# Mixed values through four buffers, two in PSUM and two in SBUF, and GpSimd's low parts of the weights in eight pieces

## What is computed

```python
h = rms_norm(x, g)
h_prev = pad(h)[:, :-1];  hh = h_prev - h
xr, xw, xk, xv, xa, xg = (h + hh * mu[i] for i in range(6))
r = xr @ w_r;  k = xk @ w_k;  v = xv @ w_v
w = -softplus(-(w0 + tanh(xw @ w1) @ w2)) - 0.5
a = sigmoid(a0 + (xa @ a1) @ a2)
g = sigmoid(xg @ g1) @ g2
kk = k * k_k, normalised by head;  k = k * (1 + (a - 1) * k_a)
```

## Time and profile before

| | us |
|---|---|
| median of three runs | 2355.26 |
| the runs | 2349.63, 2355.26, 2356.2 |
| profiled execution | 2347.22 |
| its span | 2345.3 |

### The profile page before, as it was taken

The page is one execution under the profiler, slowest core; times in us unless marked ns, Lnnn a source line. Parts: engine busy times, 40 slices in busy tenths (PEclk is TensorE's granted clock), DMA queues, the critical chain, the costliest instruction groups (busy, mean ns, idle before and its releaser), DMA issues.

```text
span 2345.3 us, 36157 instructions
## 1 busy us (share of the span) xinstructions
PE 2057.7 (88%) x15556; PEld 1574.6 (67%) x15556; DVE 848.4 (36%) x1209; ACT 809.4 (35%) x1051; POOL 686.6 (29%) x198
## 2 busy tenths in 40 slices
PE   4687886667999999989998789999998999979997
PEld 2564766663678888866665457888887886747764
DVE  5578443323342221033646724222101234252333
ACT  4566323323243342132124534434212423232232
POOL 1141322201234434423220023343443423203430
PEclk8898899997799999999997879999999998989999
DMA  4111100002123332222110012333323221112110
GB/s 146 36 36 48 41 4 4 4 4 65 46 80 90 94 100 88 98 69 97 54 54 19 1 37 80 98 89 94 99 99 103 79 66 36 54 59 90 54 54 36
DMA packets 190703, 147.06 MB, mean 63 GB/s; under 512 B 6889, under 2 KB 188352, under 8 KB 190577
## 3 DMA queue, kind: packets, MB, share of 16 engines
q1 hardware_dynamic: 190576, 145.18, 20.2%
HBM read 143.06 MB, written 2.10 MB: 62 GB/s over the span
## 4 chain that ended last, share of the span: by engine, by line
PE 76%; DVE 12%; ACT 6%; issue 4%; POOL 1%; DMA 1%; SPq 0%; DVEq 0%; ACTq 0%
PE psum L2296 20%; PE psum L2298 19%; PE psum L2297 19%; PE psum L2459 4%; DVE X_lo L1670 2%; PE psum L2372 1%; ACT w_hi L1149 1%; PE psum L2721 1%; DVE xf L1796 1%; PE psum L2302 1%; PE psum L2684 1%; POOL w_lo L1017 1%; DVE col L2071 1%; PE psum L2878 1%; ACT xf L1181 1%
## 5 line engine op out<-in xcount | busy, mean ns | idle before, releaser
L1017 POOL TENSOR_TENSOR w_lo<-weight_raw,w_hi 128x2048 fp32r<-128x2048 f32 (+2 forms) x134 | 600.7, 4484 | 1384.9 <-ACT w_hi L1149 1384.7
L2296 PE MATMUL psum<-X_hi,w_hi 128*128 128x512 f32 x1528 | 630.7, 413 | 60.4 <-DVE X_lo L1670 42.2
L2298 PE MATMUL psum<-X_hi,w_lo 128*128 128x512 f32 x1528 | 606.0, 397 | 0.0
L2297 PE MATMUL psum<-X_lo,w_hi 128*128 128x512 f32 x1528 | 605.5, 396 | 0.0
L2296 PEld LDWEIGHTS psum<-X_hi,w_hi 128*128 128x128 f32 x1528 | 293.5, 192 | 173.6 <-issue 94.4
L1149 ACT ACTIVATE w_hi<-weight_raw 128x2048 fp32r<-128x2048 f32 (+2 forms) x134 | 249.5, 1863 | 367.0 <-PE psum L2298 356.2
L2297 PEld LDWEIGHTS psum<-X_lo,w_hi 128*128 128x128 f32 x1528 | 293.8, 192 | 64.0 <-issue 6.7
L2298 PEld LDWEIGHTS psum<-X_hi,w_lo 128*128 128x128 f32 x1528 | 293.0, 192 | 64.2
L1719 DVE TENSOR_TENSOR sgate<-rt,psum 128x512 f32<-128x512 f32 x44 | 30.2, 687 | 320.5 <-PE psum L2298 320.5
L2296 PE MATMUL psum<-hb_hi,w_hi 128*128 128x512 f32 x352 | 136.9, 389 | 0.0
L2297 PE MATMUL psum<-hb_lo,w_hi 128*128 128x512 f32 x352 | 136.9, 389 | 0.0
(11 more groups left out here) (439 smaller groups left out, 2702.0 us busy)
## 6 DMA issues: line engine op xcount, KB each, us to landing
weight_raw<-in_ffn_w_gu SPq DMA_DIRECT2D x88, 512.0 KB, 4.9
weight_raw<-in_l_w_in SPq DMA_DIRECT2D x45, 512.0 KB, 4.7
weight_raw<-in_ffn_w_down SPq DMA_DIRECT2D x40, 512.0 KB, 3.6
weight_raw<-in_kv_w SPq DMA_DIRECT2D x16, 512.0 KB, 4.0
weight_raw<-in_l_w_out SPq DMA_DIRECT2D x16, 512.0 KB, 4.0
weight_raw<-in_rw_w_k SPq DMA_DIRECT2D x8, 512.0 KB, 6.7
weight_raw<-in_rw_w_r SPq DMA_DIRECT2D x8, 512.0 KB, 4.1
weight_raw<-in_rw_w_v SPq DMA_DIRECT2D x8, 512.0 KB, 4.5
```

The costliest lines, as they stand in the source:

```text
L1017: ins = pool.tensor_tensor(l, r, h.bitcast(F32), ALU.subtract)
L2296: pe.matmul(ps, wh, xh, start=start, stop=False, skip_group_check=True)
L2297: pe.matmul(ps, wh, xl, start=False, stop=False, skip_group_check=True)
L2298: return pe.matmul(ps, wl, xh, start=False, stop=stop, skip_group_check=True)
```

## The change

Two things change.

1. Mixed values before `y` (the inputs of k, r, g1 and v) and the ring's go through one set of four buffers, `mixed_at(i)`: PSUM bank 6, `xf[:, 0]`, PSUM bank 7, `xf[:, 1]`, by i modulo 4. `ring_f` is gone. The waits are relaxed to match: a buffer of tile i is free with the low part of tile i − 4. ScalarE writes the first halves two tiles ahead, and `ring_first(0)` and `ring_first(1)` stand before `keys_out(0)`. The jobs `second` and `kinv` move from banks 6 and 7 to banks 4 and 5.
2. GpSimd's subtraction for each weight slot is issued as pieces: eight of 256 columns for a full slot (six for one of 1536; eight of 160 or of 128 where the slot has three dimensions). Only the last piece counts the semaphore up, so TensorE waits for all of them. This holds for all slots, the hardware loops included.

```diff
@@ make_jobs
-        j.add(("second", m), 6 + m % 2, "A")
+        j.add(("second", m), 4 + m % 2, "A")
...
-        j.add(("kinv", k), 6 + k % 2, "D")
+        j.add(("kinv", k), 4 + k % 2, "D")
@@ new function
+def pieces(r):
+
+    if len(r.shape) == 3:
+        return [r[:, k:k + 1, :] for k in range(r.shape[1])]
+    return [r[:, c:c + 256] for c in range(0, r.shape[1], 256)]
@@ new function in build
+        def mixed_at(i):
+
+            return (psum[:, 6, :], xf[:, 0, :], psum[:, 7, :], xf[:, 1, :])[i % 4]
@@ low
-                for i, (r, h, l) in enumerate(parts):
-                    ins = pool.tensor_tensor(l, r, h.bitcast(F32), ALU.subtract)
+                for i, part in enumerate(parts):
+                    for r, h, l in zip(*(pieces(q) for q in part)):
+                        ins = pool.tensor_tensor(l, r, h.bitcast(F32), ALU.subtract)
@@ x_high1 and x_low1
+                if src is None:
+                    f = mixed_at(k) if v < XV["y"] else xf[:, k % 2, :]
+                else:
+                    f = src[:, k, :]
@@ mix_first
-                if i >= 2:
-                    act.wait_ge(xlo_ready, i - 1)
-                act.activation(xf[:, i % 2, :], h_sb[:, k, 1:S + 1], ACT.Copy,
+                if v == 1 and k < 4:
+                    act.wait_ge(ring_xl, 2 * KT - 3 + k)
+                elif i >= 4:
+                    act.wait_ge(xlo_ready, i - 3)
+                act.activation(mixed_at(k), h_sb[:, k, 1:S + 1], ACT.Copy,
@@ mix_high
                 mix_first(v, mu, 0)
+                mix_first(v, mu, 1)
                 for k in range(KT):
-                    if k + 1 < KT:
-                        mix_first(v, mu, k + 1)
+                    if k + 2 < KT:
+                        mix_first(v, mu, k + 2)
@@ ring_first
-                if j >= RING:
-                    act.wait_ge(ring_xl, j - RING + 1)
+                if j < 4:
+                    act.wait_ge(xlo_ready, KT - 3 + j)
+                else:
+                    act.wait_ge(ring_xl, j - 3)
-                act.activation(ring_f[j % RING][:, :], h_sb[:, j % KT, 1:S + 1], ACT.Copy,
+                act.activation(mixed_at(j), h_sb[:, j % KT, 1:S + 1], ACT.Copy,
@@ ring_high
-                if j + 1 < 2 * KT:
-                    ring_first(j + 1)
+                if j + 2 < 2 * KT:
+                    ring_first(j + 2)
@@ ScalarE's order
             ring_first(0)
+            ring_first(1)
             keys_out(0)
@@ split
-                    if 8 * v + k >= 2:
-                        dve.wait_ge(xlo_ready, 8 * v + k - 1)
-                    produce(k, xf[:, (8 * v + k) % 2, :]).then_inc(xf_ready, 1)
+                    if 8 * v + k >= 4:
+                        dve.wait_ge(xlo_ready, 8 * v + k - (3 if v < XV["y"] else 1))
+                    produce(k, mixed_at(k) if v < XV["y"] else xf[:, k % 2, :]).then_inc(xf_ready, 1)
```

More of the change, by code:

```diff
@@ L632, in build @@
         first_hi, first_lo = b_("first_hi", [P, KT, P], F32R), b_("first_lo", [P, KT, P], F32R)
-        ring_f = [b_(f"ring_f{i}", [P, S]) for i in range(2)]
         b_ = here(u0_at)
         ring_hi, ring_lo = b_("ring_hi", [P, RING, S], F32R), b_("ring_lo", [P, RING, S], F32R)
-        ring_f += [b_("ring_f2", [P, S])]
         b_ = here(rf_at + size([P, 2, S], F32))
@@ L1166, in x_high1 @@
                     act.wait_ge(kstep, xv_last_k(v - 1, k))
-                act.activation(X_hi[:, k, :], src[:, k, :] if src is not None else xf[:, (8 * v + k) % 2, :],
-                               ACT.Copy).then_inc(xhi_ready, 1)
+                if src is None:
+                    f = mixed_at(k) if v < XV["y"] else xf[:, k % 2, :]
+                else:
+                    f = src[:, k, :]
+                act.activation(X_hi[:, k, :], f, ACT.Copy).then_inc(xhi_ready, 1)
             def x_high(v, src=None):
@@ L1300, in ring_high @@
                     wait_ring_used(act, j - RING)
-                act.activation(ring_hi[:, j % RING, :], ring_f[j % RING][:, :], ACT.Copy).then_inc(ring_xh, 1)
+                act.activation(ring_hi[:, j % RING, :], mixed_at(j), ACT.Copy).then_inc(ring_xh, 1)
             def low_rank(n, func):
@@ L1668, in x_low1 @@
                 dve.wait_ge(xhi_ready, xready(v, k))
-                f = src[:, k, :] if src is not None else xf[:, (8 * v + k) % 2, :]
+                if src is None:
+                    f = mixed_at(k) if v < XV["y"] else xf[:, k % 2, :]
+                else:
+                    f = src[:, k, :]
                 dve.tensor_tensor(X_lo[:, k, :], f, X_hi[:, k, :].bitcast(F32), ALU.subtract).then_inc(xlo_ready, 1)
@@ L1842, in ring_low @@
                 dve.wait_ge(ring_xh, j + 1)
-                dve.tensor_tensor(ring_lo[:, j % RING, :], ring_f[j % RING][:, :], ring_hi[:, j % RING, :].bitcast(F32),
+                dve.tensor_tensor(ring_lo[:, j % RING, :], mixed_at(j), ring_hi[:, j % RING, :].bitcast(F32),
                                   ALU.subtract).then_inc(ring_xl, 1)
@@ L1851, in _ @@
             for j in range(2 * KT):
-                f, mu = ring_f[j % RING], 8 * (MU_W, MU_A)[j // KT] + j % KT
+                f, mu = mixed_at(j), 8 * (MU_W, MU_A)[j // KT] + j % KT
                 dve.wait_ge(ring_half, j + 1)
-                dve.scalar_tensor_tensor(out=f[:, :], in0=h_sb[:, j % KT, 0:S], scalar=pcol("rw_mu", mu), in1=f[:, :],
+                dve.scalar_tensor_tensor(out=f, in0=h_sb[:, j % KT, 0:S], scalar=pcol("rw_mu", mu), in1=f,
                                          op0=ALU.mult, op1=ALU.add).then_inc(ring_mixed, 1)
```

## The result

Five runs of the changed kernel have a median of 2336.82 us (2331.47 to 2339.69); the kernel before, run beside them and counted with the runs shown ahead of the prediction, has 2349.63 (2345.78 to 2356.2). The ratio is 0.9937, 95% interval 0.9913 to 0.996: about 15 us faster (9 to 20 by the interval; the medians are 12.8 us apart). The profiled executions are 2347.22 before and 2339.69 after, 7.5 us apart; the one before is faster than the median of every series of the kernel before, and the one after is the slowest of its five.

The account below looks back on a forecast made before the run. TensorE is busy 88% of 2345.3 us, so only its waits can be won; early −31.8, late −10.4 and piece cost +25.9 sum to −16.3 us: 2331 against the profiled execution, 2339 us on the median, range 2326 to 2361.

Parts of the forecast that it names:

- Start: Before the first product: DVE's three tiny instructions and h_sb tiles get in between pieces, first product at 40.2, −4.4 us.
- First step of k: Product k's first step: two tiles further ahead, mixed tiles come every 1.43 us instead of 2.28, −3.2 us.
- Ring waits: TensorE's three waits for ring_lo, 24.4 us together: −3.8 for the first, −7.5 for the other two, leaving 13.
- Product r: Product r, where DVE and GpSimd are both full: −5.2 us by its end, from mixed tiles made two ahead.
- the rival of the saturated stretch: Early stretch already full, DVE 32.99 of 35 us in r; gains given back, no change, 2356 us; chance 0.15.
- g1 and v: Products g1 and v: shorter tile pitches and, in v, xf ready 3.6 us earlier; −2.1 and −5.6 us.
- The loops: The FFN loops: 20 steps where w_lo has no slack pay 1.0 us each, +20 us; pair period 22.04 becomes 23.0.
- the four late slots: Slots in e and o products of the last layers with under 0.2 us of slack: +1.0, +1.0, +1.4 and +2.5.
- en_lo: At 1967.53, before a TensorE restart: −1.8 us in pieces, −4 more if the idle becomes too short for the clock to drop.
- The five other stretched instructions: Late DVE instructions right before a wait of TensorE, worth 0.5 to 1.7 us each: −4.6 us together.
- the dearer boundary: Rival: pieces cost more at 20 FFN steps and four late slots; at 1.8 us a slot, 2364 us; chance 0.09.
- the missing service: Rival: DVE isn't served between pieces, only the four buffers gain; +8 us, 2363; chance 0.10.

Follow-up runs that it names:

- buffers only: The changed kernel's four buffers and two tiles ahead, with every w_lo whole as in the kernel before: median 2339.14 us, ratio 0.9917.
- r1 whole: The run with chosen pieces, with the w_lo of slot r1 left whole: median 2310.69 us, ratio 0.9828.
- chosen pieces: The changed kernel with pieces only for the first 13 weight slots (k, r, g1, v) and slots kk0, kv3, ega1, oq0: median 2310.52 us, ratio 0.981.
- early pieces: The changed kernel with pieces only for the first 13 weight slots (k, r, g1, v), whole w_lo from g2 on: median 2326.92 us, ratio 0.9859.
- shifted rotation: The run with buffers only (whole w_lo), with the buffer order moved by one to SBUF, PSUM, SBUF, PSUM: median 2325.03 us, ratio 0.99.
- pieces only: The kernel before with w_lo in eight pieces and still two buffers: median 2356.91 us, ratio 1.001.
- slot k1 later: The run with chosen pieces, with GpSimd waiting for the eighth h_sb before it starts slot k1's w_lo: median 2307.07 us, ratio 0.9828.
- slot v0 whole too: The run with slot k1 later, with the w_lo of slot v0 left whole as well: median 2315.72 us, ratio 0.9837.
- 128-column pieces: The changed kernel with pieces of 512 columns up to slot 39, 128 in the second gate-up loop, 256 elsewhere: one run, 2349.3 us.

## Why the prediction was right

Forecast 2339 us against 2336.8, and 16.3 us against about 15 by the ratio. That the totals meet within 2 us is partly luck: the interval of the measured gain is 9 to 20 us, executions of one kernel lie up to 20 us apart, and the stated range, 2326 to 2361, takes in a kernel that changed nothing. What bears the prediction out is the steps, from the profiled executions:

- Start: −4.4 forecast, −5.3 measured. First step of k: −3.2, and −3.4 (k0 to k1). Ring waits: 13 forecast, 13.0 measured; by k3 −18.9 and −19.6. One reading in it was wrong: the first wait's −3.8 was put down to the pieces, and the making of tiles 0 and 1 ahead was said to add nothing while w_lo is the stall. With buffers only, all w_lo whole, this wait falls as far (7.43 to 3.53), and with the tile in SBUF only to 6.8.
- Product r and the rest to v1: −12.9 forecast, −10.6 measured. The step that was oversized is r: 5.2 us taken and 1.4 measured (k3 −19.6, g1 −21.0, where 24.1 was forecast). r1's w_lo took 10.56 us and TensorE waited 4.48 for it (timeline of 140 to 152 us of the changed kernel):

```profile
140.53 10.56 POOL L1027 TENSOR_TENSOR w_lo<-weight_raw,w_hi 128x256 fp32r<-128x256 f32 x8
...
151.15 0.80 PE L2318 MATMUL psum<-X_hi,w_hi 128*128 128x512 f32 x1 [4.48 <-POOL w_lo L1027]
```

  DVE was busy for 16.68 and GpSimd for 14.87 of the 17.75 us before that matmul, as the rival of the saturated stretch had it, and leaving r1 whole gains nothing by g1. But not all of the shortfall is that: the chosen pieces, whose instructions are the same up to v3, win 3.0 in this step (−19.0 to −22.0), and their clock after the third ring wait was 0.76 where the change's was 0.50. g1 and v made up for part: −9.2 where −7.7 was forecast. In all −30.2 against −31.8.
- The loops: +20 forecast, 10.1 + 9.7 = +19.8 measured; pair period 23.0 as forecast. Its price, 0.14 us a further piece, was read from four fp32 pieces of another line and held for fp32r ones at four, eight and sixteen.
- Three of the four late slots: +4.9 forecast by eu0, +4.1 measured, of which 1.5 to 1.7 are lost by buffers only, early and chosen pieces as well, with these slots whole (the shifted rotation loses none); the fourth, ok0, +1.0 as forecast. en_lo: −5.8 with the clock's part, −5.7 measured, and this is the best of several: with the same pieces the chosen pieces win 4.4 and the pieces only 2.9 there, and of the kernels with the slot whole two win 1.1 and 1.2 and the shifted rotation nothing. So the pieces are worth about 3 (4.4 less 1.2), and how much the clock adds changes from one execution to the next. The five other stretched instructions: −4.6 forecast; −2.8 measured between the two loops and −2.1 at L1756 of the kernel before (slot oq0), with what else changes there counted in.
- What no step had: +4.8 us between ega1 and eo0, +1.0 between v1 and the first loop, and some 2.5 in parts of about 1 us or less behind eo0. With them the profiled pair is 7.5 us apart and not 16. The 4.8 are TensorE's clock (window tables from ega1's first matmul to eo0's, in which TensorE is never idle for the first 20 us; before, after, and the run with slot k1 later):

```profile
1986.92:2020.42 33.50, 29.10 (x133) 21.60 (x133) 13.60 (x18) 7.86 (x13) 4.60 (x1) 0.95 0.10 32
```
```profile
1973.12:2011.42 38.30, 33.90 (x134) 25.31 (x133) 10.82 (x18) 7.66 (x12) 6.13 (x8) 0.80 0.09 28
```
```profile
1947.91:1979.88 31.97, 27.57 (x133) 20.55 (x133) 13.60 (x18) 7.87 (x13) 4.60 (x1) 1.00 0.10 34
```

They don't belong to the change: buffers only and early pieces, with the same instructions as before from ega0 to eo0, lose 4.7 and 4.8 in the same place, and the shifted rotation loses nothing; of the kernels with ega1 in pieces, chosen pieces lose 1.6, pieces only and slot k1 later win 1.5, and slot v0 whole too loses 4.8. How much of it the medians carry isn't shown.

Of the rivals, the dearer boundary and the missing service are refuted (0.14 us, and omu in 0.19 us). Of the signs, w_lo's waits "about 12 us a layer in place of 4" read 23.6 in the same view, since TensorE's own ten waits (9.7 us) are added to the weight load's ten (13.9); the pair period is the sum's measure and came out. The Trainium skill (SBUF — State Buffer, Who interferes with whom) has the lock last for the whole instruction and spares DVE instructions with at most one SBUF input; the runs agree for the mixed values (0.76 against 3.79 us). The prediction gave that rule too narrowly, as only for two inputs in SBUF: omu has one and took 3.25 us. The Trainium skill (SBUF — State Buffer, Who interferes with whom) excepts the 2-port perf modes, which a `tensor_scalar` like omu can enter; no run here shows in which mode omu ran. For the price of a piece, the Trainium skill (GPSIMD Engine Reference, Performance versus the Vector engine) has 156 ns of dispatch for DVE and two dispatch hops for GpSimd where DVE has one; the runs show 141 to 143 ns for each further piece on GpSimd. The pieces' pitch in w_lo is 0.695 us, 0.68 forecast.

## What to carry to other kernels

Cutting this GpSimd subtraction let VectorE in at each cut and cost 0.14 us a cut: cut only where a VectorE instruction with both inputs in SBUF is held up before a wait of TensorE, and leave it whole where the low part itself is what TensorE waits for. Here the same change with every slot behind v left whole is 18 us better, and with four late slots cut as well 30 us. When more tiles are buffered, ask which of them meet the long instruction: in the shifted rotation, the two tiles that lie in PSUM wait 3.3 and 3.9 us less and the one that lies in SBUF 3.3 more.

## What the runs showed of the hardware that was not expected

- **The same wait, two clocks.** In the second loop of the run with 128-column pieces TensorE has an idle time of 2.57 us before its restart, always the same. In 8 such restarts in a row, every second one is followed by matmuls of 0.63 us for part of the step, and its pair takes 26.23 us instead of 24.62. After the idle times of 0.97 us in the change's loops it isn't seen (pairs of 23.02 to 23.08 us). So 1.6 us more of waiting than in the change cost 2.4 us a pair in the mean, and a price per piece read from small numbers of pieces undersizes a large number: the loop lost 31.6 us where 10 × 2.6 = 26 was expected. The 4.42 us of the third ring wait are followed by clocks of 0.76 and of 0.50 in the same way (see the run with slot k1 later).
- **The spread between executions.** The kernel before ran in 2340.5 to 2360.1 us in one series of 11. Profiled executions of kernels that don't differ there take 31.97 to 38.3 us from ega1 to eo0, with mean clocks of 1.00 to 0.80. The runs with slot k1 later and with slot v0 whole too have the same instructions from v1 on; their profiled executions are 1.4 us apart at v1 and 11.1 at the end. A trace of one execution can't settle a question of 5 us by its end; the start times of single slots, in stretches with the same clock, are the better measure.
- **Alternation.** At the start, where both engines always have the next instruction ready, one piece of 256 columns and one VectorE instruction of 512 columns together take 1.13 us (1.09 in the mean of the eight h_sb tiles with the chosen pieces, 8.71 us in all), while back to back alone they take 0.68 and 0.67 (h_sb before: eight in 5.39 us). The sum would be 1.35: each is held up for a part of the other's time, not for the whole.
